# Moving the 8-block product and ScalarE's roundings in a gated delta-rule trunk

## The reference: what is computed

```python
x = x + 0.5 * swiglu(rmsnorm(x), w_gate, w_up, w_down)          # width 2816
q|k|v|g_out|a|b|glu|gates = rmsnorm(x) @ w_in
y_A = (rmsnorm(delta(silu(conv4(q,k,v)), decay, beta)) * silu(g_out)) @ w_a_out   # 8 heads x 128
y_B = silu(rmsnorm(conv31(val * sigmoid(gt)) + b)) @ w_b_out
x = x + (sigmoid(gate_A) * y_A + sigmoid(gate_B) * y_B) @ w_o
x = x + 0.5 * swiglu(...)
```

## Time and profile before

| | us |
|---|---|
| median of 3 runs | 2732.45 (2731.99 to 2735.13) |
| profiled execution, its own time | 2736.78 |
| its span | 2735.0 |
| TensorE busy in the span | 2680.4 (98%) |
| VectorE busy | 1601.0 (59%) |
| ScalarE busy | 1100.4 (40%) |

### The profile page before, as it was taken

One profiled execution on the slowest core, in us unless ns is written; L12 is line 12 of the kernel. 1 busy time (PEld: TensorE's weight loads), 2 busy tenths in 40 slices (PEclk: granted clock), 3 DMA queues, 4 the chain that ended last, 5 costly groups with the idle time before them and its releaser, 6 DMA issues.

```text
span 2735.0 us, 35214 instructions
## 1 busy us (share of the span) xinstructions
PE 2680.4 (98%) x12744; PEld 2225.1 (81%) x12744; DVE 1601.0 (59%) x2697; ACT 1100.4 (40%) x1817; POOL 254.9 (9%) x231
## 2 busy tenths in 40 slices
PE   9999999999999999999999999999999999999998
PEld 7888877888878888888888888788888788888887
DVE  6554367888885345553355543678888853455532
ACT  4222246666653242222222223566666532322222
POOL 0000022122110010000000000211211200100000
PEclk9999999999999999999999999999999999999999
DMA  4323335564543323323332333455556432333231
GB/s 165 97 95 101 98 102 130 125 144 114 132 112 100 95 89 100 100 93 100 95 99 92 100 92 100 111 122 133 124 130 139 100 100 92 100 93 100 91 98 66
DMA packets 83481, 291.87 MB, mean 107 GB/s; under 512 B 10033, under 2 KB 10801, under 8 KB 83377
## 3 DMA queue, kind: packets, MB, share of 16 engines
q1 hardware_dynamic: 68112, 235.72, 27.6%
q0 software_dynamic: 14976, 54.53, 10.9%
q10 hardware_dynamic: 288, 0.27, 0.0%
HBM read 233.86 MB, written 2.10 MB: 86 GB/s over the span
## 4 chain that ended last, share of the span: by engine, by line
PE 90%; DVE 6%; ACT 3%; issue 1%; DMA 0%; DVEq 0%; SPq 0%; POOLq 0%; POOL 0%; ACTq 0%
PE bank L462 88%; DVE cacc L1570 1%; DVE NT L1733 1%; PE bank L661 1%; ACT X L1144 1%; PE bank L709 1%; DVE dec L1713 0%; ACT cacc L1122 0%; ACT w_hi L875 0%; ACT cacc L1123 0%; DVE qa L1474 0%; DVE c_all L1573 0%; DVE ssq L1777 0%; DVE qT L1705 0%; DVE c_raw L1602 0%
## 5 line engine op out<-in xcount | busy, mean ns | idle before, releaser
L1272 DVE TENSOR_TENSOR w_lo<-raw,w_hi 128x1024 fp32r<-128x1024 f32 x342 | 422.8, 1237 | 535.6 <-ACT w_hi L875 535.4
L875 ACT ACTIVATE w_hi<-raw 128x1024 fp32r<-128x1024 f32 x446 | 469.8, 1055 | 651.2 <-PE bank L462 651.1
L462 PE MATMUL bank<-h_hi,w_hi 128*128 128x512 f32 x1504 | 588.1, 391 | 0.7 <-DVE h_lo L1297 0.4
L462 PE MATMUL bank<-h_hi,w_lo 128*128 128x512 f32 x1504 | 586.2, 390 | 0.0
L462 PE MATMUL bank<-h_lo,w_hi 128*128 128x512 f32 x1504 | 586.0, 390 | 0.0
L462 PE MATMUL bank<-g_hi,w_hi 128*128 128x512 f32 x928 | 380.0, 409 | 0.0
L462 PE MATMUL bank<-g_hi,w_lo 128*128 128x512 f32 x928 | 379.9, 409 | 0.0
L462 PE MATMUL bank<-g_lo,w_hi 128*128 128x512 f32 x928 | 371.2, 400 | 0.0
L1570 DVE SCALAR_TENSOR_TENSOR cacc<-c_raw,ncol,cacc 128x512 f32<-128x512 f32 x464 | 335.4, 745 | 14.0 <-ACT cacc L1123 13.6
L462 PEld LDWEIGHTS bank<-h_hi,w_hi 128*128 128x128 f32 x1504 | 282.4, 188 | 62.2 <-issue 1.9
L462 PEld LDWEIGHTS bank<-h_hi,w_lo 128*128 128x128 f32 x1504 | 282.4, 188 | 58.7
(11 more groups left out here) (260 smaller groups left out, 3280.9 us busy)
## 6 DMA issues: line engine op xcount, KB each, us to landing
raw<-in_w_in SPq DMA_DIRECT2D x128, 512.0 KB, 3.6
w_lo<-raw POOLq DMA_DIRECT2D x104, 512.0 KB, 4.6
raw<-in_ffn_w_up SPq DMA_DIRECT2D x88, 512.0 KB, 3.5
raw<-in_ffn_w_gate SPq DMA_DIRECT2D x87, 512.0 KB, 3.5
raw<-in_ffn_w_down SPq DMA_DIRECT2D x64, 512.0 KB, 3.5
raw<-in_ffn_w_down SPq DMA_DIRECT2D x32, 384.0 KB, 3.1
raw<-in_w_a_out SPq DMA_DIRECT2D x16, 512.0 KB, 3.5
raw<-in_w_b_out SPq DMA_DIRECT2D x16, 512.0 KB, 3.6
```

The lines of the kernel that those rows point to most:

```text
L462: return nc.tensor.matmul(o, a, b, start=start, stop=stop, **kw)
L875: nc.scalar.activation(w_hi[c % SLOTS][:, :], raw[c % SLOTS][:, :], ACT.Copy).then_inc(hi_done, 1)
L1272: tt(w_lo[c % SLOTS][:, :], raw[c % SLOTS][:, :], w_hi[c % SLOTS][:, :].bitcast(F32), ALU.subtract).then_inc(lo_v, 1)
```

## The change

`PE_ORDER`: `rows` stands three halves later, behind `vt`; `fb` with it. ScalarE: `hi` of c0+4 stands ahead of `halves(2)` and its `negative` behind `turned(2)`; one of the first taps stands on each side of `turned(3)`; the tile step t = 1 and `hi` of c0+5 change places with `halves(4)` and `turned(4)`; `vs` moves behind `XF`, `negative(c0+5)` behind `XTF`, and `hi` of c0+6 after that. VectorE: `olo` stands one level later with a tap in its place, and in the first head the tail names stand for nothing.

```diff
-PE_ORDER = "H H gr kt H kk kq H so H H H rows vt H H H H H H fb H H H H H H H H".split()
+PE_ORDER = "H H gr kt H kk kq H so H H H vt H H H rows H H H H H H fb H H H H H".split()
...
-ACT_AFTER = {1: ["n3"], 2: ["n5"] * (BASE == 1), 4: ["vs"]}
...
-    ACT_STEPS += [f"XO{_l}", f"XE{_l}", f"XT{_l}"] + ACT_AFTER.get(_l, [])
-ACT_STEPS += ["XF", "XTF", "qsq"]
+    ACT_STEPS += [f"XO{_l}", f"XE{_l}", f"XT{_l}"]
+ACT_STEPS += ["XF", "vs", "XTF", "qsq"]
...
-                    def first_taps():
+                    def first_tap(j):
...
                     dense_steps(0, *dense)
+                    hi(Rd, c0 + 4)
                     halves(2)
                     turned(2)
-                    hi(Rd, c0 + 4, residue=True)
+                    negative(c0 + 4)
                     halves(3)
+                    first_tap(0)
                     turned(3)
-                    first_taps()
+                    first_tap(1)
+                    dense_steps(1, *dense)
+                    halves(4)
                     if before:
                         o_round(rn - 1)
+                    turned(4)
                     squares(0, 1)
-                    dense_steps(1, *dense)
                     hi(Rd, c0 + 5)
-                    halves(4)
-                    turned(4)
-                    negative(c0 + 5)
+                    halves(5)
+                    turned(5)
+                    dense_steps(2, *dense)
+                    pe_(f"xy{LEVELS - 1}")
+                    nc.scalar.activation(X[:, :], bank[0][:, :], ACT.Copy).then_inc(*ac_dn.step("XF"))
                     act.wait_ge(po_dn.sem, po_dn.after(rn, "rk"))
                     pe_("vt")
                     act.wait_ge(ac_dn.sem, ac_dn.after(rn, "ksq"))
                     for c in range(NC):
                         a = nc.scalar.activation(vs[:, c * P:c * P + P], bank[4][:, c * P:c * P + P], ACT.Copy, scale=sm[:, 3, c:c + 1])
                     a.then_inc(*ac_dn.step("vs"))
-                    halves(5)
-                    turned(5)
-                    squares(2, 3)
-                    dense_steps(2, *dense)
-                    hi(Rd, c0 + 6)
-                    pe_(f"xy{LEVELS - 1}")
-                    nc.scalar.activation(X[:, :], bank[0][:, :], ACT.Copy).then_inc(*ac_dn.step("XF"))
-                    negative(c0 + 6)
                     pe_("xtf")
                     nc.scalar.activation(XT[:, :], bank[3][:, :], ACT.Copy).then_inc(*ac_dn.step("XTF"))
+                    negative(c0 + 5)
+                    squares(2, 3)
+                    hi(Rd, c0 + 6, residue=True)
                     dense_steps(3, *dense)
...
-                    behind = {2: ("l", "c", "a", "oF", (0, 0)), 3: ((0, 1), "t", (0, 2), "olo", "t"), 4: ((1, 0), "t", (1, 1), "t", (1, 2)),
+                    behind = {2: ("l", "c", "a", "oF", (0, 0)), 3: ((0, 1), "t", (0, 2), "t", "t"), 4: ((1, 0), "t", (1, 1), "olo", (1, 2)),
...
-                            if x == "t" or x in DVE_TAIL and not (dn and before):
+                            if x == "t":
                                 fill()
                             elif x in DVE_TAIL:
-                                tail(x, rn - 1, hn - 1)
+                                if before:
+                                    tail(x, rn - 1, hn - 1)
```

More of the change, by code:

```diff
@@ L1117, in odd_columns @@
                         nc.scalar.activation(packed(*NO[lv], lv), alternate(NT, lv, 1), ACT.Copy).then_inc(*ac_dn.step(f"n{lv}"))
-                    def first_taps():
-                        act.wait_ge(ve_cr.sem, ve_cr.after(rn, "craw"))
-                        nc.scalar.activation(cacc[0][:, :], c_raw[:, 0:SEQ], ACT.Identity, bias=ncol[:, PR_B:PR_B + 1], scale=ncol[:, 0:1]).then_inc(taps, 1)
-                        nc.scalar.activation(cacc[1][:, :], c_raw[:, 1:1 + SEQ], ACT.Copy, scale=ncol[:, 1:2]).then_inc(taps, 1)
+                    def first_tap(j):
+                        if j == 0:
+                            act.wait_ge(ve_cr.sem, ve_cr.after(rn, "craw"))
+                            nc.scalar.activation(cacc[0][:, :], c_raw[:, 0:SEQ], ACT.Identity, bias=ncol[:, PR_B:PR_B + 1], scale=ncol[:, 0:1]).then_inc(taps, 1)
+                        else:
+                            nc.scalar.activation(cacc[1][:, :], c_raw[:, 1:1 + SEQ], ACT.Copy, scale=ncol[:, 1:2]).then_inc(taps, 1)
                     def squares(*ms):
```

## The result

Before 2733.61 us (median of 4 runs), after 2693.01 us (2691.95 to 2693.14, 4 runs): ratio 0.9851, 95% interval 0.9836 to 0.9866. That is 40.6 us against the 42.9 forecast, and 3.5 us above the predicted time. The profiled executions, 2736.78 and 2693.10 us, differ by 43.7 us. TensorE's idle time fell from 54.6 to 21.3 us, and its busy time by 10.4.

The account below looks back on a forecast made before the run. TensorE, busy 98% of the span, was taken as the bound, with its waits to be removed. Middle heads 25.7 + first 14.0 + last 3.2 = 42.9 us, off 2732.45 gives 2689.5 us; range 2680 to 2706.

Parts of the forecast that it names:

- four names of the earlier trace: TensorE's waits holding nearly all its idle time: `rows` for `own`, `xt` for `XO`, `xy` for `YD`, layer end for a sum.
- A middle head, 2.14 us: Gain in each of 12 middle heads: 0.85 us from `rows` plus 1.29 from `XO` of level 4, 25.7 in all.
- new stall at level 2: In a middle head `xt` would wait 0.41 us for the later `XO`, costing 0.64 with its restart.
- Rival A: No new stall at level 2 if `near_inverse` makes up 0.46 us: 9 us more gained, 2680.5 us; chance 0.12.
- A first head, 7.0 us: Gain per layer's first head: 3.47 us to level 2, 3.32 from level 3 to 4, 0.2 behind; 14.0 in all.
- A last head, 1.6 us: Gain per layer's last head: VectorE's tap ahead of `YD` of level 3 comes 1.6 us earlier; twice, 3.2 us.
- signs of being right: No middle-head wait for `own`; 0.2 to 0.4 us for `XO` at level 2, none at level 4; first-head clock 1.00.
- sign of being wrong: A TensorE wait at the start of tile t = 5, or `YD` of level 2 or 3 among the waits.
- Costed at nothing: Moves of `hi` of c0+4, `vs`, `fb`, `olo` and `negative` of c0+5, claimed to delay nothing that TensorE needs.
- cover of 1.6 us: Transfer of c0+5, issued at about 597.0, lands at 601.6; TensorE needs it for tile t = 5 at 603.2.
- By idle entries or by starts: TensorE's stalls priced by idle entries would sum to about 32 us; priced from start to start, 43 us.
- the start of the sum: Gain subtracted from the 2732.45 us median, though read from a 2736.78 us execution; none of the 4.3 between placed in these stages.

Follow-up runs that it names:

- e1: Kernel before with TensorE's order alone changed (`rows` and `fb` three halves later); 2717.05 us, ratio to before 0.9934.
- e2: Kernel before with ScalarE's order alone changed, TensorE's list and VectorE's tables as before; 2711.74 us, ratio to before 0.9916.
- e5: Kernel after, but with `rows` and `fb` two halves later instead of three; 2688.97 us, ratio to before 0.9833.
- e3: Kernel before with only VectorE's first-head table changed, so tail names stand for nothing instead of a tap; 2731.85 us, ratio to before 0.9985.
- e7: Kernel after, but `negative(c0+5)` 1.43 us later, behind the rounding of c0+6 and tile step t = 3; 2696.19 us, ratio to before 0.9859.
- e8: Kernel after, but `negative(c0+5)` also behind the rounding of c0+7, 2.4 us later than in the change; 2712.78 us, ratio to before 0.9922.

## Why the prediction was right

- **What bounds.** Right. Three of the four names of the earlier trace rows, with the half-clock stretches behind them, held all the gain: 44.1 us in the stretches of heads, 0.4 lost outside. The fourth, the sum, stayed at 4.0 us as forecast.
- **A middle head, 2.14 us.** Measured 2.20. `rows` on its own 0.89 (0.85 forecast, e1), `XO` of level 4 on its own 1.31 (1.29, e2). The new stall at level 2 was there: in the timeline after, `xt` waits for `XO`, which stands 0.44 us ahead of it, as it did at level 4 before. e5 removes it. Rival A is refuted in the main: `rows` started 0.52 us later, `near_inverse` 0.40 and `XO` 0.40. The 0.12 made up is at the start, where a tap had stood before, as that rival had it; the chain itself makes up nothing.
- **A first head, 7.0 us.** Measured 7.06 in layer 1, 6.97 in layer 2. From `gr` to `xt` of level 2 it gained 3.41 us (3.47 forecast), from there to level 4 3.33 (3.32), and 0.3 behind that. The parts aren't independent, as the text had them: in e3 the second falls short without ScalarE's new order. About 3.4 us of the 7 are the clock's, two half-clock stretches of about 1.7 us each in the profiled execution. In single executions they are missing with either order alone too (e1 in layer 1, e2), and perhaps in some of the kernel before (see below).
- **A last head, 1.6 us.** Measured 2.03 and 1.99; the mis-sized term. The tap came 1.6 us earlier, as forecast. Behind it the last head's own stall at level 4, which the prediction didn't count, is gone too. `XO` is in time: `xt` starts 0.14 us sooner behind `xy` of level 3, `y` follows `xt` after 0.22 us instead of 0.37, and 0.1 more comes behind.
- **The signs.** All signs of being right came, but for the size of the wait at level 2 (0.53 us in the weight loads). One sign of being wrong came as well: `YD` of level 3 is still among the waits, 0.45 us in each last head, down from 1.18. The prediction's own step for that head left it there, since `YD` came only 1.6 us earlier.
- **Costed at nothing.** `hi` of c0+4, `vs`, `fb` and `olo` show in no wait. The transfer of c0+5 was issued at 537.88, 596.96 in the old count (597.0 forecast), and its cover of 1.6 us is confirmed by e7 and e8 to within a few tenths. The queue behind it was taken too lightly: the median landing of the 104 remainders rose from 4.6 to 5.2 us and the longest from 6.8 to 10.1. No wait came of it, since those are needed in the next head.
- **By idle entries or by starts.** The idle entries of these waits, less the new stall, gave 32 us, starts 43, measured 44 in the stage. Only about half of the 12 us between is restart. The other 6.8 us are the four half-clock stretches of the first heads, which is TensorE running slower and not an effect of pipelining. The Trainium skill ("Perfetto Trace Analysis", section "Identifying the Most-Contended Engine") calls matmul busy time a bad measure of what is left. The trace agrees: for the same 12744 matmuls the busy time fell by 10.4 us, part of it the clock's.
- **3.5 us above the predicted time.** The heads gained 1.2 us more than forecast, so the terms don't explain it. What does is the start of the sum: the gain was read from an execution of 2736.78 us and taken off a median of 2732.45, on the claim that no part of these 4.3 us is in the heads. No row bore that claim. In 13 later runs the median was 2735.06; against it the change is worth 42 us. The scatter of the kernel before goes with the clock. Of the 20 later runs the four fastest (2730.4 to 2731.9 us) have a mean granted clock of 0.996 or 0.997, the eight above 2736 us one of 0.994 or 0.995. The profiled execution (0.995) has the four half-clock stretches, 6.8 us together, in its first heads; the four runs after all have 0.997. So the faster executions of before probably lacked some of these stretches and had less to gain. Where the clock fell in them isn't on record.

## What to carry to other kernels

Price a stall of an engine in program order from start to start of its instructions, not by its idle entry, and carry the delay of the moved product to the next wait in the chain before you count the gain. Take the gain off the execution from which it was read, or price the clock's share by itself: it isn't the same in every execution. A product moved behind filler work should move just as far as its input is late: one filler more and the stall only changes its name (e5 against the change, 4 us). A stall that is removed may uncover one behind it on the same engine (e3), so a change of three parts is to be measured by leaving each out as well as by doing each alone.

## What the runs showed that I had not expected

The clock did not follow the length of a stall. In the kernel before, the first head's 1.86 us wait was followed by a stretch at 0.50, TensorE's 1.2 GHz level; in e2 the same wait, 1.87 us at the same place, by none, in both layers:

```profile
419.00:421.00 2.00, 2.00 (x11) 1.73 (x12) 1.07 (x7) 2.00 (x5) 0.00 (x0) 1.00 0.45 121
421.00:423.00 2.00, 2.00 (x11) 1.63 (x10) 1.73 (x9) 1.05 (x3) 0.92 (x1) 1.00 0.40 150
```

In e1 the 1.8 us wait for `YD` left the clock alone in layer 1 (first head 48.03 us) and not in layer 2 (49.62). In e8 waits of 1.6 and 1.8 us left it alone too. Behind the 4.0 us wait at the end of a layer the clock fell every time, but not for the same length: in layer 2 it was back sooner before than after (granted clock of the 5 and 4 us around the sum, first before, then after), which is the 0.9 us that the last stretch loses.

```profile
2172.00:2177.00 5.00, 3.87 (x15) 3.30 (x16) 3.47 (x5) 2.27 (x4) 2.53 (x2) 0.71 0.00 0
2177.00:2181.00 4.00, 4.00 (x24) 3.36 (x23) 2.79 (x3) 1.09 (x2) 0.30 (x1) 0.94 0.74 218
```

```profile
2127.00:2132.00 5.00, 3.45 (x12) 3.17 (x13) 2.34 (x5) 2.55 (x4) 1.30 (x2) 0.51 0.00 1
2132.00:2136.00 4.00, 4.00 (x17) 3.16 (x17) 3.17 (x3) 0.00 (x0) 1.54 (x1) 0.76 0.54 144
```

What decides it stays open; these runs tell only that a stall of 1.8 or 1.9 us may or may not cost 1.7 us more. And one packet of an instruction fetch of 0.02 MB beside the remainder transfer of c0+5 goes with a landing 0.6 to 1.2 us later in the middle heads of e7 and e8, which a cover of half a microsecond doesn't survive. That the packet is the cause was seen side by side, not tested.
